# Scores of two heads together and a rounded bias product in the softmax stages of a one-core transformer kernel

## The reference, cut to what matters

```python
# "forget": 8 heads of 64, in each of the two layers of the first block
c = jnp.cumsum(log_f, axis=1).transpose(0, 2, 1)          # log_f = log_sigmoid(fl + b_forget), 8 heads
z = jnp.einsum('bthd,bshd->bhts', qb, kf) * scale
z = z + cb[..., None] - c[:, :, None, :]                  # the forget bias
p = jax.nn.softmax(jnp.where(causal, z, -jnp.inf), axis=-1)
# "sparse": 8 heads of 64, in each of the two layers, over the keys that an index branch has chosen (top 64)
z = jnp.where(valid, einsum(q, k_sel) * scale, -jnp.inf);  p = softmax(z)
# "swa": 16 heads of 64 with a window of 128 keys, in the last layer
s = einsum('bnqkgd,bnskd->bnkgqs', q, kb) * (SWA_HEAD_DIM ** -0.5)
p = jax.nn.softmax(jnp.concatenate([where(mask, s + bias, -inf), sink], axis=-1), axis=-1)[..., :-1]
```

## Time and profile before

| what | value |
| --- | --- |
| median of three runs (lowest, highest) | 2611.24 us (2606.49, 2626.17) |
| the profiled execution | 2605.32 us, of which the span from first to last instruction is 2603.5 |
| TensorE (PE) busy | 2487.0 us, 96% of the span |
| VectorE (DVE) busy | 1755.4 us, 67% |
| ScalarE (ACT) busy | 1419.3 us, 55% |
| GpSimd (POOL) busy | 136.5 us, 5% |
| mean granted TensorE clock | 0.977 of 2.4 GHz |
| HBM read | 580.13 MB, 224 GB/s over the span |

### The profile page before, as it was taken

The page is one execution under the profiler, slowest core; times in us unless marked ns, Lnnn a source line. Parts: engine busy times, 40 slices in busy tenths (PEclk is TensorE's granted clock), DMA queues, the critical chain, the costliest instruction groups (busy, mean ns, idle before and its releaser), DMA issues. The chain is left out here.

```text
span 2603.5 us, 34769 instructions
## 1 busy us (share of the span) xinstructions
PE 2487.0 (96%) x13881; PEld 2106.1 (81%) x13881; DVE 1755.4 (67%) x2013; ACT 1419.3 (55%) x1625; POOL 136.5 (5%) x176
## 2 busy tenths in 40 slices
PE   6999999999998999999999897999999999999996
PEld 6786789888866998878899786888888888888885
DVE  3345655544466555666544557898989898988987
ACT  3543544454345444523434445777777777777775
POOL 0101200001022000042000000000000000000000
PEclk9999999999999999899999997999999999999998
DMA  8232355532424455604555426999999999999996
GB/s 282 98 135 97 131 187 178 193 138 102 161 99 162 170 194 179 116 1 133 173 181 194 138 65 203 365 367 365 358 364 366 360 359 362 365 356 358 368 363 226
DMA packets 391569, 586.60 MB, mean 225 GB/s; under 512 B 21168, under 2 KB 284656, under 8 KB 391280
## 3 DMA queue, kind: packets, MB, share of 16 engines
q1 hardware_dynamic: 391408, 584.37, 66.3%
HBM read 580.13 MB, written 4.19 MB: 224 GB/s over the span
## 5 line engine op out<-in xcount | busy, mean ns | idle before, releaser
L3378 DVE TENSOR_TENSOR moe_low<-ring,moe_high 128x2048 fp32r<-128x2048 f32 x288 | 658.9, 2290 | 96.3 <-ACT moe_high L3339 92.4
L3339 ACT CAST moe_high<-ring 128x2048 fp32r<-128x2048 f32 x288 | 548.8, 1908 | 154.0 <-PE bank L3263 81.2
L3263 PE MATMUL bank<-moe_high,moe_xh 128*128 128x512 f32 x896 | 240.6, 390 | 7.9 <-PEq L3088 7.9
L3263 PE MATMUL bank<-moe_high,moe_xl 128*128 128x512 f32 x896 | 240.3, 390 | 0.0
L3263 PE MATMUL bank<-moe_low,moe_xh 128*128 128x512 f32 x896 | 240.1, 390 | 0.0
L3263 PEld LDWEIGHTS bank<-moe_high,moe_xh 128*128 128x128 f32 x896 | 168.4, 188 | 43.1 <-issue 8.1
L3263 PEld LDWEIGHTS bank<-moe_high,moe_xl 128*128 128x128 f32 x896 | 168.7, 188 | 35.2
L3263 PEld LDWEIGHTS bank<-moe_low,moe_xh 128*128 128x128 f32 x896 | 168.5, 188 | 35.1
L2048 DVE TENSOR_TENSOR chain_low<-ring,chain_high 128x2048 fp32r<-128x2048 f32 x48 | 110.0, 2292 | 127.3 <-ACT chain_high L2021 127.3
L2021 ACT CAST chain_high<-ring 128x2048 fp32r<-128x2048 f32 x44 | 83.8, 1904 | 151.9 <-PE bank L1992 116.9
L3269 PE MATMUL bank<-moe_high,moe_hh 128*128 128x512 f32 x448 | 128.4, 408 | 2.3 <-DVE moe_hl L3383 2.3
(11 more groups left out here) (513 smaller groups left out, 4993.6 us busy)
## 6 DMA issues: line engine op xcount, KB each, us to landing
ring<-in_moe_w_gate SPq DMA_DIRECT2D x199, 512.0 KB, 5.7
ring<-in_moe_w_up SPq DMA_DIRECT2D x199, 512.0 KB, 7.4
ring<-in_moe_w_down SPq DMA_DIRECT2D x95, 1024.0 KB, 7.9
ring<-in_w_in SPq DMA_DIRECT2D x22, 2048.0 KB, 8.0
ring<-in_w_down SPq DMA_DIRECT2D x14, 2048.0 KB, 7.9
ring<-in_w_up SPq DMA_DIRECT2D x10, 2048.0 KB, 8.1
xT<-in_moe_w_down SPq DMA_DIRECT2D x18, 1024.0 KB, 7.7
xT<-in_moe_w_gate SPq DMA_DIRECT2D x31, 512.0 KB, 5.7
```

What stands on the lines that cost most here:

```text
L3263: mm = pe.matmul(core.banks[i % 2][:], (xl if other_low else xh)[:, place(m), 4 * part + c, :], wt[:, c, :], start=(part == 0 and j == 0 a ...
L3339: act.copy(unit(high, u), ring.raw(u)).then_inc(s["weight_high"], 1)
L3378: dve.tensor_tensor(unit(low, u), ring.raw(u), unit(high, u), ALU.subtract)\
```

## The change

1. **Scores of two heads at a time.** In even iterations the TensorE program issues the scores of heads i and i + 1: the 128-column products of both, then the 256-column products of both. The two heads lie in different halves of the array's rows and write different banks. Odd iterations have no scores. The wait for `masked` now is for head i - 1 to have left its bank, and stands in even iterations only.
2. **The forget bias as one rounded product.** `cum` becomes a 72-row fp32r tensor `forget_sums`. Rows 0 to 7 hold the sums rounded, rows 32 to 39 the rounded rest, rows 64 to 71 what is left after both. The stationary operand is `thirds`, 72 x 8, with ones where the row modulo 32 is the head. An fp32 product of 8 rows (two records) becomes an fp32r product of 72 rows (one record), and in a pair of heads the two bias products of equal width follow each other. To make the three parts, VectorE writes its sum three times into a zeroed buffer (L1493 in the new numbering), the row sums of TensorE come out 72 wide, and five VectorE instructions stand where one copy did (L1498 to L1505).
3. **Two unread products per head instead of four** in swa.
4. Memory: `LOWER` falls from 7168 to 6976 words, 8 columns are added to the constants, and `rest` takes 256 words of the lower scratch.

```diff
-LOWER, UPPER, UPPER_BC = 7168, 6144, 5248
+LOWER, UPPER, UPPER_BC = 6976, 6144, 5248
...
+        "thirds": (p % 32 == np.arange(8)[None, :]) & (p < 72),
...
         for i in range(heads + 3):
-            h = i
-            if h < heads:
-                if h >= 2:
-                    pe.wait_ge(s["masked"], h - 1)
-                bank = core.banks[h % 2]
+            if i < heads and i % 2 == 0:
+                both = (i, i + 1)
+                if i >= 2:
+                    pe.wait_ge(s["masked"], i)
                 for t, (a, b) in enumerate(edges):
-                    mm = pe.matmul(bank[:, a:b], q(h)[:, t * P:(t + 1) * P], k(h)[:, 0:b - a],
-                                   start=True, stop=(bias is None))
-                    if bias is not None:
-                        mm = pe.matmul(bank[:, a:b], bias_lhs(h), bias_rhs[:, 0:b - a], start=False, stop=True)
-                mm.then_inc(s["scores"], 1)
+                    for h in both:
+                        mm = pe.matmul(core.banks[h % 2][:, a:b], q(h)[:, t * P:(t + 1) * P], k(h)[:, 0:b - a],
+                                       start=True, stop=(bias is None))
+                        if bias is None and t == NT - 1:
+                            mm.then_inc(s["scores"], 1)
+                    for h in both if bias is not None else ():
+                        mm = pe.matmul(core.banks[h % 2][:, a:b], bias_lhs(h), bias_rhs[:, 0:b - a], start=False, stop=True)
+                        if t == NT - 1:
+                            mm.then_inc(s["scores"], 1)
...
-                idle_products(core, pe, core.banks[2 + i % 2][:, TRI:BANK], 4)
+                idle_products(core, pe, core.banks[2 + i % 2][:, TRI:BANK], 2)
...
+            dve.memset(self.flat, 0.0).then_inc(s["step"], 1)
+            dve.tensor_copy(self.pick, core.const("thirds")[0:self.ROWS, :]).then_inc(s["step"], 1)
         if u == 19:
...
-            dve.tensor_tensor(self.u, self.u, e, ALU.add).then_inc(s["step"], 1)
+            for n in range(3):
+                dve.tensor_tensor(self.spread[:, :, 32 * n:32 * n + 8], self.u2, self.e2, ALU.add).then_inc(s["step"], 1)
         if u == 21:
+            sums = core.banks[6][0:self.ROWS, 0:T]
+            rest = self.rest[0:self.ROWS, :]
             dve.wait_ge(s["sums"], 1)
-            dve.tensor_copy(self.cum[0:8, :], core.banks[6][0:8, 0:T]).then_inc(s["cum"], 1)
+            dve.tensor_copy(self.bias, sums).then_inc(s["step"], 1)
+            dve.wait_ge(s["step"], 9)
+            dve.tensor_tensor(rest, sums, self.bias, ALU.subtract).then_inc(s["step"], 1)
+            dve.wait_ge(s["step"], 10)
+            dve.tensor_copy(self.bias[32:64, :], rest[32:64, :]).then_inc(s["step"], 1)
+            dve.tensor_copy(self.bias[64:72, :], rest[64:72, :]).then_inc(s["step"], 1)
+            dve.wait_ge(s["step"], 12)
+            dve.tensor_tensor(self.bias[64:72, :], rest[64:72, :], self.bias[64:72, :], ALU.subtract).then_inc(s["cum"], 1)
             self.logits.rest(dve, 0)
```

More of the change, by code:

```diff
@@ L1423, with __init__ @@
     LOADS = 6
-    def __init__(self, core, rows, turned, fl, b, cum, tmp, logits):
-        self.core, self.rows, self.turned, self.fl, self.b, self.cum, self.logits = core, rows, turned, fl, b, cum, logits
+    ROWS = 72
+    def __init__(self, core, rows, turned, fl, b, cum, tmp, rest, logits):
+        self.core, self.rows, self.turned, self.fl, self.b, self.rest, self.logits = core, rows, turned, fl, b, rest, logits
         self.u, self.e = tmp[:, 8:24], tmp[:, 24:40]
-        self.u2 = self.u.rearrange("p (t h) -> p t h", t=NT)
+        self.u2, self.e2 = (a.rearrange("p (t h) -> p t h", t=NT) for a in (self.u, self.e))
+        self.flat = tmp[:, 40:40 + NT * self.ROWS]
+        self.spread = self.flat.rearrange("p (t h) -> p t h", t=NT)
+        self.bias = cum[0:self.ROWS, :]
+        self.pick = core.thirds[0:self.ROWS, :]
         self.s = {n: core.sem(f"first_{n}") for n in ("turned", "step", "log", "sums", "cum")}
@@ L1439, in pe @@
         if u == 20:
[L1440 to L1444, removed]
+            pe.wait_ge(s["step"], 5 + 3)
+            bank = core.banks[6][0:self.ROWS]
+            pe.matmul(bank[:, 0:P], self.spread[:, 0, :], core.const("le"), start=True, stop=True)
+            pe.matmul(bank[:, P:T], self.spread[:, 0, :], core.const("ones"), start=True, stop=False)
+            pe.matmul(bank[:, P:T], self.spread[:, 1, :], core.const("le"), start=False, stop=True).then_inc(s["sums"], 1)
     def act(self, act, u, act_stored, dve_stored):
@@ L2093, in head_rows, with later_branches @@
     return lambda h: x[HD * (h % 2):HD * (h % 2) + HD, chunk(h), :]
-def later_branches(core, w, i, base, projections, of_projections, side, branches, br, qT, kT, v, cum, tmp, logits, gates, parts):
+def later_branches(core, w, i, base, projections, of_projections, side, branches, br, qT, kT, v, tmp, logits, gates, parts):
     scratch = LOWER + 4 * BANK
@@ L2108, in later_branches @@
         lambda h, t: core.const("neg")[:, P * t:P + 2 * P * t], br,
-        bias=(lambda h: core.const("ident")[0:8, h:h + 1].broadcast_to([8, P]), cum[0:8, :]), logits=gates[0], rope=rope,
+        bias=(lambda h: side.pick[:, h:h + 1].broadcast_to([side.ROWS, P]), side.bias), logits=gates[0], rope=rope,
         behind=BehindProjections(of_projections, side, branches))
@@ L2135, in attention @@
     br, at = core.part(at, NT, BW)
-    cum, at = core.part(at, T)
     tmp, at = core.part(at, 320)
+    rest, at = core.part(at, T)
     with core.scratch("upper_a", UPPER, LOWER):
@@ L2142, in c_cols @@
         return core.cproj[:, :, j * BW:min(C_COLS, (j + 1) * BW)]
-    with core.first_unit(f"attention{i}"), core.scratch("upper_bc", UPPER_BC, LOWER):
+    with core.first_unit(f"attention{i}"), core.scratch("upper_bc", UPPER_BC, LOWER), \
+            ExitStack() as memory:
+        cum = memory.enter_context(core.nc.sbuf_tensor(f"forget_sums{i}", [P, T], F32R))[:]
         parts = Parts(core)
@@ L2147, in attention @@
         gates = [SplitLogits(core, "forget", w, base + 11, logits[1], 0, parts, 0, 0, led=True)]
-        side = FirstTurn(core, br, branches, core.cproj[:, :, 0:8], core.b_forget[:, i, :], cum, tmp, gates[0])
+        side = FirstTurn(core, br, branches, core.cproj[:, :, 0:8], core.b_forget[:, i, :], cum, tmp, rest, gates[0])
         projections, of_projections = split_projection_part(core, "bc_proj", w, [
@@ L2153, in attention @@
             beside=lambda pool: clear(pool, sems), side=side)
-        later_branches(core, w, i, base, projections, of_projections, side, branches, br, qT, kT, v, cum, tmp, logits, gates,
+        later_branches(core, w, i, base, projections, of_projections, side, branches, br, qT, kT, v, tmp, logits, gates,
                        parts)
@@ L2253, in build @@
         core.bias_there = core.sem("bias_there")
+        core.thirds = core.sbuf("thirds", [P, KC], F32R)
         core.angle_room = core.sbuf("angle_room", [P, 36])
```

2 lines of the change are left out of this document (1 added, 1 removed).

## The result

Median 2530.79 us (2525.05 to 2533.68, four runs) against 2609.35 for the kernel before in the same session; the ratio is 0.9685, interval 0.9649 to 0.9721. The kernel is faster by 3.15%, some 79 us, where 2562 us, 42.7 off, was forecast and 2550 was the lower end. The profiled execution took 2525.05 us, its span 2523.3.

What follows compares the result with a forecast made beforehand. The prediction took TensorE's instruction list to bound the softmax stages. Savings of 19.4 us in forget, 8.0 in sparse and 15.3 in swa made 42.7 off the profiled 2605.3, so 2562 us, range 2550 to 2580.

Steps and rivals of the forecast that it cites:

- what bounds the stages: Softmax stages: each as long as TensorE's instruction list; what comes off it comes off the time, until VectorE's or ScalarE's work.
- The start's wait: Start of swa: the third head waits until both first heads are masked, so TensorE waits about 1.3 us.
- VectorE's two-head backlog: Pairs: the wait for masked refers to heads scored two iterations ago; the second head's transposes come two iterations later.
- the chain ahead of forget: Before forget: VectorE's five instructions take 2.6 us of the 3.6 available, so they were costed at nothing.
- two halves side by side: Paired scores: two heads in different row halves run together, costing as one head plus 0.01 us for the offset.
- the first rival: Paired scores and bias: halves overlap less (2570, none 2578) or narrow rounded product is slow (2569); chance 0.17.
- two and a change: 0.43: Forget: two rounded bias products at 0.12 us each plus one change of rows at 0.19.
- the clock in layer one: Layer one's forget: a drop to 1.2 GHz cost 4.6 us; if it does not return, 2558 us.
- the clock falls in swa: Swa: unread products only keep the engine busy; at 1.2 GHz throughout 33 us more, 2595; chance 0.07.
- The sum: Whole kernel: 19.4 + 8.0 + 15.3 = 42.7 us off the profiled 2605.3 gives 2562.6, stated as 2562.
- TensorE's need per head in sparse: Sparse after the change: TensorE would need 2.86 us per head.
- "slower" rival: All five softmax stages, about 147 us, stay at 1.2 GHz, costing 142 us more: 2705; chance 0.02.

Runs made afterwards that it cites:

- kernel 8: The changed kernel with one head's scores at a time and four unread products, keeping the rounded bias and new places: 2565.79 us, ratio 0.9805.
- kernel 5: The kernel before with two unread products per head instead of four in swa, nothing else: 2595.29 us, ratio 0.9931.
- kernel 1: The kernel before with 64 unused bytes a partition behind b_forget, giving x the changed kernel's address: 2594.00 us, ratio 0.9939.
- kernel 2: The changed kernel with 64 more unused bytes a partition behind b_forget, distance 0: 2548.34 us, ratio 0.9764.
- 3: The kernel before with the weight parts 64 bytes lower and x where it was: 2587.53 us, ratio 0.9899.
- 7: The kernel before with scores of two heads at a time and 64 unused bytes behind b_forget, bias still fp32: 2547.28 us, ratio 0.9738.
- 9: The changed kernel with 32 more bytes a partition ahead of what follows thirds, distance 32: 2553.84 us, ratio 0.9769.
- 4: The kernel before with scores of two heads at a time alone, fp32 bias and four unread products kept: 2573.14 us, ratio 0.9866.

## Why the prediction was off

**Right: what bounds the stages.** All five became shorter by what was taken off TensorE's list. Sparse gave 3.85 and 4.26 us (8.1 for 8.0 forecast), swa 15.45 (15.3), with the pair at 3.88 us (3.9), the iteration behind the last scores at 1.44 (1.42). The start's wait was 0.74 us, not 1.3: the second head's maximum came sooner. VectorE's two-head backlog did no harm: no wait before transposes appears, and 0.7 us in all before value products, as before.

**Right: the chain ahead of forget costs nothing.** 1.96 us instead of the 2.6 estimated, with 1.46 us to spare. The casts of 32 and 8 rows take 0.28 us, less than the 0.41 charged.

**Right: two halves side by side**, and so the first rival (2570, 2578) was not met. Pairs alone took 8.0 us off swa (48.71 - 40.76), with the head's 0.99 us of scores paid once a pair. The Trainium skill, "TensorE: Matmul & The Clock Gate", section "Packing small matmuls — row/col tiling", would have the pair start and end in program order. The trace disagrees, and the clearest case is stick before the change: there the other head's 256-column product starts 13 to 14 ns behind the first head's, at 87.63 us, and the first head's 128-column product, which stands between the two in the code, starts at 88.16. In the changed kernel the two products of one width are neighbours in the code, and their records start 6 to 7 ns apart; a width takes two steps, not three.

**Mis-sized: the bias term in forget.** The step "two and a change: 0.43" charged 0.19 us for each change of rows, a value read off fp32 products. In the new pair the bias group takes 0.36 us at 128 columns (179.88 - 179.52) and 0.34 at 256 (180.86 - 180.52); the scores take 0.42 and 0.64, as forecast. The block is 1.76 us instead of 1.92, the pair 6.58 instead of 6.8. By kernel 8, a single rounded product costs 0.25 and 0.22, so the second adds 0.11 to 0.12, as the 256-column row it was read from says, and 0.10 to 0.13 are left for the change of rows instead of 0.19. Which of the two changes around such a product is the cheaper one, the records do not say. As a mean over the four changes of a head it is 0.16 us in kernel 8 (1.52 less 0.22, 0.12, 0.43 and 0.12 for the products), where the old sequence has 0.19 to 0.20. In layer two, 10.7 us were gained for 9.7 forecast: 2 us in the two layers.

**Too small a chance: the clock in layer one.** The 4.6 us were seen and left out of the sum. They came: 41.65 - 36.99 = 4.7. That it was layer one's 4.6 is chance, since in kernel 5's profile the drop stood in layer two. That there is a drop to win back is not: the old forget sequence is prone to it in every profile taken (up to 30.7 us at half clock in one stage, kernel 1), and the changed one had none in any. The rival "the clock falls in swa" did not occur with two unread products; with none it did, for 6.8 us.

**Failed: that the rest stays.** "The sum" took every stage outside for unchanged, and part 4 of the change, the memory, was costed at nothing without being named. It is the largest miss, 30.6 us between the two profiles. Added up from each product's start to the next, with what the half clock lost taken apart, the rest of the span is made of:

| us in the rest | before | after | kernel 2 |
| --- | --- | --- | --- |
| x's products of 256 columns | 586.9 | 566.3 | 591.4 |
| x's products of 512 columns | 110.8 | 109.3 | 109.0 |
| MLP's products of 512 columns | 239.7 | 236.1 | 234.6 |
| lost to the half clock | 55.5 | 47.5 | 52.8 |
| more than 0.5 us to the next start, mostly waits | 105.7 | 109.0 | 104.6 |

So 20.6 us come from x's products of 256 columns, 5.1 from the products of 512, and 8.0 from less time at half clock; 3.3 were given back as waits, and 0.2 is all other products. Against kernel 2, 23.3 us hang on the 64 bytes: 25.1 less in x's products and 5.3 in the half clock, against 4.4 more in waits, 1.5 in the MLP's products and 1.2 elsewhere. The other 7.3 us lie between distances 128 and 0 (2418.7 - 2411.4): there x's products of 256 columns are 4.5 slower, while the MLP's win 5.1, x's of 512 columns 1.8, the clock 2.7 and everything else 2.2. What the 64 bytes do is shown by kernels 1, 2, 3, 7 and 9; why the distance matters to the engine stays open, and so does how much of the 8.0 us of clock belongs to the change and how much to the executions that were profiled.

Together: 42.7 forecast, 2 for the bias, 4.7 for the clock, 0.2 in swa and sparse make 49.6, and 30.6 for the rest 80.2, the difference of the two spans (2603.5 - 2523.3).

**Slips in the working.** TensorE's need per head in sparse is 2.88 us by the prediction's own terms, not 2.86. In the "slower" rival the five stages add up to the 142 us that it charges (about 32, 27, 25, 25 and 33), not to the 147 written ahead of it. Neither enters the forecast.

## What to carry to other kernels

An edit that widens a tensor moves all that is allocated behind it. Where a kernel lives on long runs of products of two SBUF operands, compare the start-to-start time of an untouched product, before and after, ahead of crediting a gain to the edit; and try a pad of 64 bytes by itself, since it can be worth as much as a rewritten stage. Then judge the pad in more than one version: here it gained 17 us in one kernel (1) and 26 with pairs (7 against 4, by medians from two chips; 33 by their ratios), and by the profiles the difference is half clock in stages elsewhere.

Independent heads whose contraction fills half of the rows can be issued in alternation, and cost as one: 0.93 us for two heads' scores, 0.92 for one's.

## What was not expected of the hardware

- The rate of fp32r products went with the distance of their two operands in SBUF in all five placements tried: 113 to 120 ns at 256 columns, 227 to 234 at 512, with the weight load at 192 ns at distance 0 and at 188 or 189 elsewhere. No distance was best for both widths, and at 64 there are two paces, 113 and 118 ns, for the same addresses.
- The granted clock fell to 1.2 GHz in stages in which TensorE was busy for 100% of the time, for 23.9 and 17.1 us at a stretch (kernel 1). It didn't once the narrow fp32 products of 8 rows were gone (8), and only for 3.4 us at a stretch once the heads were paired (7). The Trainium skill, "TensorE: Matmul & The Clock Gate", section "Why this matters for your kernels", speaks of idle gaps between matmuls; no such gap stands in these windows.
- A change of rows between products has no single price: about 0.19 us between fp32 products, 0.16 on average where every second product is a rounded one.
